# Differential attention: transposes apart from the value products, head outputs in the banks of their transposes, and the scan's norm products behind the last heads' weights

## The reference, cut to what matters

```python
s = jnp.einsum("bqhcd,bkhcd->bhcqk", q_blk, k) * scale       # c = 0, 1: two score maps per head
p = jax.nn.softmax(jnp.where(mask, s, -jnp.inf), axis=-1)
w = p[:, :, 0] - lam * p[:, :, 1]
o = jnp.einsum("bhqk,bkhe->bqhe", w, v)
...
o = rmsnorm(o, subln_w) * (1.0 - lambda_init)
y_att = o.reshape(b, S, ATT_WIDTH) * jax.nn.silu(z)
y_ssd = rmsnorm(y * jax.nn.silu(z), norm_w)
y = jnp.concatenate([y_ssd, y_cfm, y_att], axis=-1)
x = x + jnp.einsum("bse,ed->bsd", y, w_out[l])
```

## Time and profile before

| | |
|---|---|
| time, median of 3 runs | 3599.92 us (3590.1 to 3601.7) |
| the profiled execution: own time, span | 3592.01 us, 3590.2 us |
| PE busy in it | 3422.2 us, 95% of the span |
| DVE busy | 1963.8 us, 55% |
| ACT busy | 548.5 us, 15% |
| POOL busy | 161.0 us, 4% |
| mean granted TensorE clock | 0.972 of full speed |
| attention, first layer: first transposes to first output tile | 2971.18 to 2996.24 us |
| attention, second layer: the same | 3469.25 to 3494.26 us |

### The profile page before, as it was taken

How to read it: one execution, slowest core, us unless ns; L and a number is a source line. 1 busy time by engine, 2 the same in 40 slices (tenths; PEclk the granted TensorE clock), 3 DMA queues, 4 the chain that set the end, 5 groups by cost and what they waited for, 6 DMA issues and landing times. The chain is left out here.

```text
span 3590.2 us, 54661 instructions
## 1 busy us (share of the span) xinstructions
PE 3422.2 (95%) x23594; PEld 2876.6 (80%) x23594; DVE 1963.8 (55%) x2748; ACT 548.5 (15%) x1032; POOL 161.0 (4%) x166
## 2 busy tenths in 40 slices
PE   6999999997989989999899999999899999999989
PEld 2445475545878879998799999999888987889978
DVE  2176762225666746551566666744475764375662
ACT  1100011223344421000100000000101122101130
POOL 0000002000000010000000000000041000060000
PEclk9999999998889999999999999999999999999999
DMA  8887723102332244444344444455444423444413
GB/s 344 312 344 314 308 103 119 58 12 71 90 76 77 58 175 160 174 176 153 117 166 173 164 171 168 173 179 186 144 143 153 155 101 119 150 144 153 157 67 129
DMA packets 134896, 559.63 MB, mean 156 GB/s; under 512 B 57552, under 2 KB 61904, under 8 KB 72256
## 3 DMA queue, kind: packets, MB, share of 16 engines
q1 hardware_dynamic: 120256, 456.17, 36.2%
q10 hardware_dynamic: 14448, 100.62, 7.1%
HBM read 539.25 MB, written 17.30 MB: 155 GB/s over the span
## 5 line engine op out<-in xcount | busy, mean ns | idle before, releaser
L470 PE MATMUL ps<-arena,ring 128*128 128x256 f32 (+2 forms) x3168 | 829.8, 425 | 27.6 <-issue 11.8
L470 PEld LDWEIGHTS ps<-arena,ring 128*128 128x128 f32 x3168 | 609.2, 193 | 246.5 <-issue 172.5
L2586 PE MATMUL ps<-arena 128*128 128x128 f32 x2560 | 292.4, 275 | 0.0
L2586 PEld LDWEIGHTS ps<-arena 128*128 128x128 f32 x2560 | 289.1, 192 | 0.0
L2586 PE MATMUL ps<-arena,ring 128*128 128x128 f32 x1920 | 220.9, 275 | 0.0
L2586 PEld LDWEIGHTS ps<-arena,ring 128*128 128x128 f32 x1920 | 217.7, 192 | 0.1
L2992 PE MATMUL ps<-arena 128*128 128x128 f32 x1792 | 204.7, 275 | 0.0
L2992 PEld LDWEIGHTS ps<-arena 128*128 128x128 f32 x1792 | 202.4, 192 | 0.0
L801 DVE SCALAR_TENSOR_TENSOR arena<-arena,small 128x512 f32<-128x512 f32 x240 | 180.5, 752 | 35.1 <-DMA arena<-in_ada_late 18.8
L3543 PE MATMUL ps<-arena,ring 128*128 128x256 f32 x832 | 180.2, 379 | 0.0
L3543 PEld LDWEIGHTS ps<-arena,ring 128*128 128x128 f32 x832 | 157.9, 190 | 22.2 <-issue 1.0
(11 more groups left out here) (509 smaller groups left out, 4394.4 us busy)
## 6 DMA issues: line engine op xcount, KB each, us to landing
ring<-in_weights SPq DMA_DIRECT2D x402, 1024.0 KB, 4.8
arena<-in_ada_late ACTq DMA_DIRECT2D x64, 1024.0 KB, 8.7
arena<-in_gates SPq DMA_DIRECT2D x56, 256.0 KB, 3.6
arena<-in_front ACTq DMA_DIRECT2D x8, 1024.0 KB, 8.9
arena<-in_x ACTq DMA_DIRECT2D x2, 2048.0 KB, 12.5
keep_g<-arena SPq DMA_DIRECT2D x14, 256.0 KB, 2.0
arena<-keep_h SPq DMA_DIRECT2D x3, 1024.0 KB, 6.5
arena<-in_ctx ACTq DMA_DIRECT2D x1, 2048.0 KB, 23.6
```

The lines of the kernel that those rows point to most:

```text
L470: mm = M.matmul(o, ring[:, slot, k, c0:c0 + w], rhs, start=(kc == 0), stop=(kc == ktiles * WK - 1))
L2586: mm = M.matmul(o, w[:, k], x(k), start=(k == 0), stop=(k == HD - 1))
```

## The change

The transposes leave `values(h)` and become `turn_over(h)`, and TensorE's order is written anew, so that other products stand between the transposes of a head and its value products. The output of head h goes to bank 4 + h % 2, the bank of its transposes, instead of bank 7. The value products no longer wait for the preceding head's copy. Instead `turn_over(2)` and `turn_over(3)` wait for the copies of heads 0 and 1. Half pieces 3 and 5 move from banks 6 and 5 to bank 7, piece 4 from 5 to 6, and the wait for the copy of piece 4 is dropped. On VectorE the maxima and mixes of heads 2 and 3, with the copies of heads 0 and 1 between them, stand ahead of the scan norm's reciprocal and its eight products, and no longer behind them. ScalarE's queue is unchanged. All of this holds for both layers.

```diff
-        PIECE_BANK = (4, 5, 6, 6, 5, 6)
+        PIECE_BANK = (4, 5, 6, 7, 6, 7)
...
-            def values(h):
+            def turn_over(h):
                 p.wait_ge(at['w_in'].sem, at['w_in'].due(p))
+                if h >= 2:
+                    p.wait_ge(at['o_in'].sem, at['o_in'].due(p))
                 for n in range(3):
                     mm = M.transpose(ps[:, 4 + h % 2, n * P:(n + 1) * P], wt[:, h % 2, n * P:(n + 1) * P], C('ident'))
                 mm.then_inc(at['t_mm'].sem, at['t_mm'].up(p))
+
+            def values(h):
                 p.wait_ge(at['t_in'].sem, at['t_in'].due(p))
-                if h >= 1:
-                    p.wait_ge(at['o_in'].sem, at['o_in'].due(p))
-                o = ps[:, 7, 0:T]
+                o = ps[:, 4 + h % 2, 0:T]
...
             copied(0)
+            turn_over(0)
+            scores(2)
             values(0)
-            scores(2)
             copied(1)
+            turn_over(1)
+            scores(3)
             values(1)
-            scores(3)
+            piece(3)
             copied(2)
-            piece(3)
             piece(4)
-            values(2)
+            turn_over(2)
             copied(3)
             piece(5)
-            copied(4)
+            turn_over(3)
+            values(2)
             values(3)
...
-                p.wait_ge(at['o_in'].sem, at['o_in'].due(p))
+                p.wait_ge(at['o_in'].sem, at['o_in'].due(p, 2))
...
-                V.tensor_copy(oa[:, h], ps[:, 7, 0:T]).then_inc(at['o_in'].sem, at['o_in'].up(v))
+                V.tensor_copy(oa[:, h], ps[:, 4 + h % 2, 0:T]).then_inc(at['o_in'].sem, at['o_in'].up(v))
...
             mix(1)
+            maxes(2)
+            maxes(3)
+            outs(0)
+            mix(2)
+            outs(1)
+            mix(3)
             rms_s[2](v, scale=False)
...
-            outs(0)
-            outs(1)
-            maxes(2)
-            maxes(3)
-            mix(2)
-            mix(3)
             outs(2)
             outs(3)
```

## The result

The changed kernel takes 3575.05 us (median of 6 runs, 3571.86 to 3580.69) against 3600.81 us before (6 runs, 3590.1 to 3605.49): ratio 0.9937, 95% interval 0.9921 to 0.9953. By this ratio it is 22.7 us less (17 to 28). The time forecast was 3583, the range 3571 to 3593. The profiled execution has a span of 3573.5 us, 16.7 less than before.

What follows compares the result with a forecast made beforehand. TensorE, busy 95% of the span, was the bound; only idle time and slow clock could be won. Savings of 8.33 and 8.28 us in the two layers, 16.6 together, off the 3599.9 median gave 3583.3 us, range 3571 to 3593.

Steps and rivals of the forecast that it cites:

- New stretch: TensorE from first transposes to first output tile in a layer's attention: 16.73 us, against 25.06 and 25.01 before.
- The wait before head 3's values: TensorE waits 0.15 us for ScalarE's copy, ready 1.23 after piece 5, with 1.08 of work between.
- margin of 0.12 for head 1: Before head 1's values, 1.18 us of TensorE work covers the 1.06 until ScalarE's copy is ready: no wait.
- four small waits: TensorE's waits before value products on ScalarE's copy, counted as four in two layers; 0.57, 0.73 and 0.73 us in the first.
- margin of 0.2 us: VectorE's norm products, last in its new queue, end at 2987.70; TensorE wants them at 2987.91 for the first output tile.
- The 1.43 us: Loss per layer from half clock: head 1's values and head 3's scores take 3.14 us for work of 1.71.
- long wait: TensorE idles 4.19 us before head 1's values, until VectorE copies head 0's out of bank 7.
- VectorE takes the place of the wait (1): VectorE is late with the norm products, up to 3 us of wait per layer: gain about 11, 3589 us; chance 0.11.
- The clock does not hold (2): Pauses between short groups drop TensorE to 1.2 GHz in the stretch, up to 6.1 us per layer: 3595.5; chance 0.04.
- Given back later (3): Second layer's start or projections wait for VectorE or weights, losing the first layer's 8.3 us: 3591.6; chance 0.05.
- Slower (4): VectorE's norm products hold up the first output tile, 7.7 us more per layer at twice the chain: 3615; chance 0.04.

Runs made afterwards that it cites:

- e8: Changed kernel with two extra VectorE products (result never read) ahead of the norm products, 2.4 us more per layer: ratio 0.9981 to the kernel before, stretches 19.10 and 18.93 us.
- e7: Kernel before with 8 TensorE products, result never read, put into the wait ahead of head 1's values: ratio 0.9984, stretches 23.55 and 23.47 us.
- e0: Kernel before, run again unchanged: ratio 0.9996, median 3594.72 us, stretches 26.48 and 24.99 us.
- second comparison: Changed kernel, unedited, timed again beside the kernel before: ratio 0.9951, 17.6 us less.
- e1: Changed kernel with VectorE put back in its old order, split and own banks kept: ratio 0.9970 to the kernel before, stretches 21.65 and 21.71 us.
- e5: Changed kernel's banks alone, with the old order on TensorE and VectorE: ratio 0.9972 to the kernel before, stretches 21.76 and 21.58 us.
- e2: Kernel before with only VectorE reordered, norm products behind mix 3; bank 7 and joint transposes and values kept: ratio 0.9977, stretches 20.02 and 20.02 us.
- e6: Changed kernel without the split, each head's values right behind its transposes: ratio 0.9967 to the kernel before, stretches 20.03 and 20.02 us.
- e9: e8 with the norm products' signal raised twice, after four products each: ratio 0.9956 to the kernel before, stretches 17.41 and 17.25 us.
- e4: Changed kernel, run again unedited: ratio 0.9951 to the kernel before, median 3577.98 us, stretches 16.75 and 16.89 us.

## Why the prediction was right

The range held, and so did the direction and the mechanism. The size is right or somewhat low: the gain was 22.7 us by the first comparison and 17.6 by the second, and 16.4 in the traces, for 16.6 forecast.

**The sum.** New stretch forecast 16.73 us, measured 16.75 and 16.89, twice. Its terms: transposes 0.32 to 0.33 (2980.09 to 2980.41, 2983.87 to 2984.20), with 0.42 in the two cases where scores follow them (2969.10 to 2969.52); the scores behind them 0.86 (2969.52 to 2970.38); values 0.76. So head 1's transposes started 2.04 us after head 0's, for 2.03 forecast. That the sum agrees to 0.02 is in part luck, since its terms err both ways: in the first layer the transposes take 1.49 instead of 1.28, and values, half pieces and the small wait together 0.19 less than forecast. The wait before head 3's values was put at 0.15: head 2's values last 0.89 (2984.20 to 2985.09) instead of 0.76, so 0.13.

**The waits.** None before heads 0, 1 and 2, as reckoned; the margin of 0.12 for head 1 was enough. ScalarE and VectorE were in time for heads 2 and 3. (The prediction speaks of four small waits in the two layers; its own rows have six, three per layer, and its sum takes them rightly.) The step that came out differently is the last. For the norm products the prediction had a margin of 0.2 us. It was 0.04 in the first layer by e8, because TensorE starts 0.17 us after VectorE has gone on, a hand-over that the sum lacked. In the second layer it was -0.14, because of the 0.60 us behind the last norm product there, where the prediction's terms had 0.24.

**The clock.** The 1.43 us as a cost apart from the wait is shown by e7, which recovers it without removing the wait's cause. But the term was read from one execution as if it were a constant. In e0 the same wait cost 1.4 us more in one of its two stretches. That is the mis-sized term: the loss behind a long wait was 1.4 to 1.6 us in three of the four stretches of the kernel before and 2.8 in the fourth. So by the stretches the change is worth 16.4 us, and about 19 if both waits cost as much as that one.

**The predicted time.** 3583 was 8 us above the median. The gain taken from the stretches was subtracted from the median of three runs. The 1.4 us more that a long wait can cost may account for part of it. The rest is probably the spread of the runs: the same two kernels gave 3577.98 and 3596.44 in the second comparison. What makes one execution of a kernel 10 us longer than another is, apart from falls of the clock like those above, not settled. Much of it lies where nothing was changed: the first stretch starts between 2964.2 and 2975.8 us in the twelve traces.

**The rivals.** VectorE takes the place of the wait (1): by 0.14 us in one layer, not 3; by e8, nearly all that VectorE gets to do more there becomes such a wait. The clock does not hold (2): refuted, 1.00 in both stretches of both traces. The Trainium skill (TensorE: Matmul & The Clock Gate, A second HAM failure mode: psum-queue depth-cycling) reports a kernel in which short idles between groups that cycle through banks made the clock fall and rise. Here some ten changes between short groups over several banks did not lower it in any of these stretches. Given back later (3): no wait grew, those between the stretches are the same 6.8 us before and after; the 1.71 us of clock there also come without the change (e0). Slower (4): the nearest to it was e1, where VectorE stayed late, and it was still faster than before.

## What to carry to other kernels

When one engine's wait ends on another engine's short instruction, look first at what stands ahead of that instruction in its queue and when that work is needed: here 5.3 us of norm products, not needed for another 18 us, stood ahead of a copy of 0.42, and to move them was 5.0 of the 8.3 us per layer. Work moved behind should arrive just in time, and its margin is the new bound. A long wait on TensorE can cost more than its length. So several short waits can be better than a long one of the same sum, as e5 against e1 suggests.

## What the runs showed of the hardware

In the attention stretches the granted clock fell to half behind the long wait in all four of the kernel before (4.00 to 4.19 us, in before and e0) and behind 3.29 and 3.13 us in e1. It did not fall behind 1.68 and 1.50 us (e5), nor behind 0.73 or 0.57 us (e2, e6), nor behind 2.19 and 2.02 us (e8).

Around 2.1 us the length of the wait doesn't decide it. Each trace has four waits of 2.05 to 2.12 us in the two layers ahead of the stretches, two in each layer. Behind the one for L3049, in the projections, the clock fell in 11 of 12 traces in the first layer and in 8 of 12 in the second (0.76 over 7 us each time). Behind the one for L3469, in the scan, some 40 us ahead of the stretch, it fell in 11 of 12 in the first layer and in only 2 of 12 in the second, e8 and e9 (0.72 over 6 us). What decides is open. A single profile doesn't show it: before and e0, the same kernel, differ by 1.7 us at one such place, although the wait there is the same to 0.01 us.

At full clock the stretches repeat to 0.01 us between executions whose total times differ by 4 us (the change and e4).
